# Mask sums of the mLSTM heads from GpSimd to VectorE, and another order of VectorE's work in a head

## The reference, cut to what matters

```python
b = jnp.cumsum(fc, axis=-1)
dmat = jnp.where(lower, b[..., :, None] - b[..., None, :] + ic[..., None, :], NEG)
...
w_intra = jnp.exp(dmat - m_t[..., None])
w_inter = jnp.exp(inter - m_t)
s = jnp.einsum('bhtd,bhsd->bhts', qc, kc) * w_intra
num = w_inter[..., None] * jnp.einsum('bhtd,bhde->bhte', qc, C) + jnp.einsum('bhts,bhse->bhte', s, vc)
den = w_inter * jnp.einsum('bhtd,bhd->bht', qc, n) + jnp.sum(s, axis=-1)
h = num / jnp.maximum(jnp.abs(den), jnp.exp(-m_t))[..., None]
...
C_new = decay[..., None, None] * C + jnp.einsum('bhs,bhsd,bhse->bhde', w_state, kc, vc)
```

## Time and profile before

| | |
|---|---|
| median of 3 runs | 1091.32 us (1090.98 to 1092.84) |
| profiled execution, its own time | 1088.49 us |
| its span in the trace | 1086.7 us |
| PE busy | 976.1 us (90%) |
| DVE busy | 634.8 us (58%) |
| ACT busy | 496.0 us (46%) |
| POOL busy | 163.8 us (15%) |
| mean granted TensorE clock | 0.956 |
| mLSTM loop (first values of head 0 to the block U) | 291.48 to 425.88 us |

### The profile page before, as it was taken

How to read it: one execution, slowest core, us unless ns; L and a number is a source line. 1 busy time by engine, 2 the same in 40 slices (tenths; PEclk the granted TensorE clock), 3 DMA queues, 4 the chain that set the end, 5 groups by cost and what they waited for, 6 DMA issues and landing times.

```text
span 1086.7 us, 14384 instructions
## 1 busy us (share of the span) xinstructions
PE 976.1 (90%) x5874; PEld 869.9 (80%) x5874; DVE 634.8 (58%) x781; ACT 496.0 (46%) x632; POOL 163.8 (15%) x151
## 2 busy tenths in 40 slices
PE   6799999999888787999999999982999999999960
PEld 2378888899888787999998998882788888888850
DVE  0645643322566767232215444536599999999986
ACT  3354343411445354222124123223578787787753
POOL 3000000010413110696000000001011111111120
PEclk9899999999989899999999999995899999999995
DMA  9735444421523303232221124521999999999945
GB/s 346 305 117 184 166 155 176 143 99 40 143 96 89 96 20 117 103 141 87 79 78 43 74 78 172 234 92 67 356 378 412 423 410 422 406 421 414 396 182 207
DMA packets 36065, 216.40 MB, mean 199 GB/s; under 512 B 4352, under 2 KB 4800, under 8 KB 15520
## 3 DMA queue, kind: packets, MB, share of 16 engines
q1 hardware_dynamic: 27024, 180.23, 42.6%
q0 software_dynamic: 8112, 32.53, 8.7%
q10 hardware_dynamic: 864, 2.73, 0.6%
HBM read 200.68 MB, written 14.79 MB: 198 GB/s over the span
## 4 chain that ended last, share of the span: by engine, by line
PE 82%; DVE 7%; DMA 5%; issue 2%; ACT 2%; SPq 0%; DVEq 0%; ACTq 0%; POOL 0%; POOLq 0%
PE ps L1505 79%; DMA rowA<-yscr 2%; DMA raw<-in_wst 2%; PE ps L1890 1%; DVE cs L1116 1%; DMA yscr<-yb,slot_rows 1%; ACT owh L695 1%; DVE xr L1483 1%; DVE rowB L1480 1%; DVE hn L970 1%; PE ps L1908 1%; DMA xg<-h2scr,slot_rows 1%; DVE hlo L983 0%; DVE hn L988 0%; DVE xr L1487 0%
## 5 line engine op out<-in xcount | busy, mean ns | idle before, releaser
L944 DVE TENSOR_TENSOR wlo<-raw,whi 128x2048 fp32r<-128x2048 f32 x37 | 85.7, 2318 | 145.9 <-ACT whi L595 145.9
L1505 PE MATMUL ps<-hhi,whi 128*128 128x320 f32 x672 | 153.8, 310 | 1.7 <-ACT gF L632 1.7
L1505 PE MATMUL ps<-hhi,wlo 128*128 128x320 f32 x672 | 153.1, 309 | 0.0
L1505 PE MATMUL ps<-hlo,whi 128*128 128x320 f32 x672 | 153.1, 309 | 0.0
L1505 PEld LDWEIGHTS ps<-hhi,whi 128*128 128x128 f32 x672 | 112.6, 188 | 4.9 <-ACT gF L632 2.0
L1505 PEld LDWEIGHTS ps<-hhi,wlo 128*128 128x128 f32 x672 | 112.4, 188 | 0.0
L1505 PEld LDWEIGHTS ps<-hlo,whi 128*128 128x128 f32 x672 | 112.3, 188 | 0.0
L595 ACT ACTIVATE whi<-raw 128x2048 fp32r<-128x2048 f32 x37 | 70.5, 1907 | 85.9 <-PE ps L1505 83.7
L1380 DVE TENSOR_TENSOR wlo<-raw,whi 128x2048 fp32r<-128x2048 f32 x32 | 72.6, 2289 | 5.6 <-ACT whi L871 5.5
L1380 DVE TENSOR_TENSOR olo<-raw,ohi 128x2048 fp32r<-128x2048 f32 x32 | 72.4, 2287 | 4.6 <-ACT ohi L871 4.6
L553 POOL DMA_INDIRECT xg<-h2scr,slot_rows x16 | 18.4, 1149 | 361.7 <-DVE slot_rows L1433 244.9
(11 more groups left out here) (342 smaller groups left out, 2253.7 us busy)
## 6 DMA issues: line engine op xcount, KB each, us to landing
raw<-in_wexp SPq DMA_DIRECT2D x64, 1024.0 KB, 8.6
raw<-in_wst SPq DMA_DIRECT2D x60, 1024.0 KB, 5.1
eraw<-in_wexp SPq DMA_DIRECT2D x32, 1024.0 KB, 7.5
nm<-negscr POOLq DMA_DIRECT2D x8, 640.0 KB, 7.5
wib<-wiscr POOLq DMA_DIRECT2D x8, 512.0 KB, 6.4
xT<-in_x SPq DMA_DIRECT2D x4, 640.0 KB, 11.1
xr<-in_xt SPq DMA_DIRECT2D x1, 2560.0 KB, 9.7
h2scr<-ht ACTq DMA_DIRECT2D x5, 512.0 KB, 3.0
```

The costliest lines, as they stand in the source:

```text
L944: dve.tensor_tensor(lo[:, :], raw[s][:, :], f32(hi[:, :]), ALU.subtract)\
L1505: return nc.tensor.matmul(out, lhsT, rhs, start=start, stop=stop)
```

## The change

The two mask sums of a head are issued by DVE in place of POOL. In DVE's loop `chunk_states(h + 1)` stands directly behind `scale_queries(h + 1)`, then come the rows of head h, then the masks of head h + 2, the products of head h + 1 and `gate_lo(h + 3)`. POOL's loop holds transfers only, the load of `wib` ahead of the one of `nm`.

```diff
@@ POOL
             gp.dma_start(stC[:, :, :, :], st_d).then_inc(d_st_wp, 16)
-            mask_maxima(0)
             gp.wait_ge(v_free, 6 + N_V * NT)
             load_inter(0)
             load_maxima(1)
             for h in range(1, H):
+                load_inter(h)
                 if h < H - 1:
                     load_maxima(h + 1)
-                mask_maxima(h)
-                load_inter(h)
@@ DVE
+            def mask_maxima(h):
+                dve.wait_ge(d_nm[h % 2], 16 * (h // 2 + 1))
+                if h:
+                    dve.wait_ge(s_exp, 2 * h)
+                for d in range(2):
+                    neg = cst[:, (C_NEGF, C_NEGB)[d]:(C_NEGF, C_NEGB)[d] + P]
+                    dve.tensor_tensor(nmd[:, d, :].rearrange("p (t n) -> p t n", n=P),
+                                      nm[h % 2][:, d, :].rearrange("p (t n) -> p t n", n=P),
+                                      by(neg.unsqueeze(1), [P, NT, P]), ALU.add).then_inc(s_mask, 1)
...
             dve.wait_ge(s_gtok, 1)
+            mask_maxima(0)
             for t in range(NT):
                 value_rows(3, t)
             products(0)
             scale_queries(0)
             chunk_states(0)
+            mask_maxima(1)
             gate_lo(2)
             for h in range(H):
                 if h < H - 1:
                     scale_queries(h + 1)
-                    products(h + 1)
-                    gate_lo(h + 3)
                     chunk_states(h + 1)
                 for t in range(NT):
                     head_rows(h, t)
+                if h < H - 2:
+                    mask_maxima(h + 2)
+                if h < H - 1:
+                    products(h + 1)
+                    gate_lo(h + 3)
```

More of the change, by code:

```diff
@@ L460, in load_inter @@
                              .partition_broadcast(P)).then_inc(d_wib, 16)
[L462 to L471, removed]
             load_maxima(0)
```

## The result

The changed kernel takes 1055.89 us (median of 4 runs, 1050.32 to 1057.19) against 1091.38 us of the kernel before (4 runs, 1090.98 to 1092.84): the ratio is 0.9663, with a 95% interval of 0.9627 to 0.9699. It is faster by about 35 us. The profiled execution took 1055.19 us with a span of 1053.4 us; before, these were 1088.49 and 1086.7 us. Between the two profiled executions the gain is 33.3 us.

A forecast was written before the change was run, and what follows sets the result against it. PE was bound by waits for `cs`, held behind `gate_lo` and ACT. Six heads 29.5 us plus tail 2.15 gave 31.7 us: profiled 1088.49 to 1056.8, median 1091.32 to 1059.6; range 1056.5 to 1067.

The forecast's parts named there:

- the last term of the sum: From profiled time to median: the profiled 1056.8 us, with 2.83 us more for the median, becomes 1059.6.
- A head without the stall: PE's time per head in the loop: 13.27 us from tile 2's restart plus 1.34, 14.61 us in place of 19.53.
- Step 1: DVE, states ahead of products and `gate_lo`: states end at 14.9 us, before tile 2 of the next values, 1 us to spare.
- Step 2: DVE's loop with the masks, 1.56 us for two: 13.6 us against PE's 14.61, so it fits.
- Step 3: ACT behind the later masks: weighted keys done at 10.9 us, needed by PE's `states` at 11.5, 0.6 us of room.
- Steps 4 and 5: Products behind DVE's rows are hidden by 4.6 us; POOL's loads of `wib` and `nm` are both hidden.
- Step 6: Tail from the values of head 6 to `U`: 15.05 us against 17.20, with PE idle some 3.9 us.
- The half clock: PE's stretches at 1.2 GHz after stalls: about 6.6 of the 29.5 us gained in six heads.
- A: Rival: DVE's or ACT's ring becomes the bound, partial gain, 1067 us; chance 0.11.
- B: Rival: PE's clock keeps falling, four of six heads keep a slow stretch of 1.64 us, 1066 us; chance 0.06.
- C: Rival: the stall reappears at another wait (`s_p`, `st_free` or `wib`), heads stay near 19.5 us, 1091 us; chance 0.01.
- D: Rival: slower, DVE's loop passes 19.53 us, the old length of a head, 1102 us; chance 0.02.

The follow-up runs named there:

- a_order_only: DVE's new order (states, rows, products, `gate_lo`) with the masks still on POOL, against the kernel before: 1057.85 us, ratio 0.9707.
- c_order_only: The new DVE order with masks still on POOL, run again on another chip, against the kernel before: 1054.41 us, ratio 0.9679.
- a_masks_only: Masks moved to DVE behind the rows, the rest of DVE's program in the old order, against the kernel before: 1089.31 us, ratio 0.9995.
- b_gate_behind: The kernel before with only `gate_lo` moved, behind the rows; masks stay on POOL: 1064.04 us, ratio 0.9782.
- b_tail: The changed kernel with the products of head 7 ahead of the rows of head 6: 1055.00 us, ratio 0.9691 to the kernel before.
- b_masks_twice: The changed kernel with each mask sum made twice: 1058.85 us, ratio 0.9738 to the kernel before.
- a_after_again: The changed kernel, unchanged, run again beside the kernel before: 1055.05 us, ratio 0.9676.
- a_before_again: The kernel before, unchanged, timed against itself: 1089.24 us, ratio 1.000.
- sets a and c: Runs whose labels begin with a or c, each set taken together on its own chip; kernel before 1089.58 us in a, 1089.61 in c.
- b_states_first: The kernel before with the states moved ahead of products and `gate_lo`, all ahead of the rows; masks on POOL: 1068.85 us, ratio 0.9840.

## Why the prediction was right, and where it failed

The mechanism and its places were right. The forecast of 1059.6 was 3.7 us too slow. 2.1 us of that come from the last term of the sum and 1.6 from the sum itself, and the range left only 0.3 us for the second.

- **What bounds the kernel.** Right: a states chain held by `gate_lo` and ACT. a_order_only and c_order_only take nearly the whole gain, a_masks_only takes none, and b_gate_behind shows that moving `gate_lo` alone gives 22.7 us, where b_tail, in the same set, gives 31.8.
- **A head without the stall.** 14.61 predicted, 14.50 measured. The 13.27 us from the restart to the next values hold a first product of 0.49 us in place of 0.39, so the restart was still in it. Six heads: 0.7 us.
- **Step 1.** Right: states ready before tile 2, no wait for `cs`.
- **Step 2.** Right: masks 1.55 (1.56 predicted), products 1.55, 1.0 us idle a head as worked out; with the masks doubled DVE becomes the bound. The contended price is real where both engines sum at once (b_gate_behind), and the change takes it away.
- **Step 3.** Right: 0.6 us of room predicted, 0.6 measured, and b_masks_twice uses it up.
- **Steps 4 and 5.** No wait for `s_p` before head 7, nor for `wib` or `nm` inside the loop. The earlier `wib` of head 1, which I put at nothing for PE, matters only where the masks stay on POOL: in a_order_only its lateness, together with the slow `qd`, costs 1.5 us.
- **Step 6.** 15.05 predicted, 14.97 measured (16.24 and 15.09 in two more traces); the gap on PE 3.9 predicted, 3.80 measured; the clock fell behind it. The 0.3 us for the clock is partly luck: in a_after_again, where it fell at once (0.79 over the tail), the tail was 1.3 us longer, and b_tail kept 1.00 through a gap of 3.02.
- **What comes later** moved as a whole: from `U` to the last expert product 619.81 us before and 619.20 after, 0.6 us less.
- **The step that failed.** "It lies 2.83 below the median of the runs, 1091.32, which would become 1059.6." This took the difference between one execution and the median of three for something that the kernel keeps. It does not: the profiled execution lay 0.2 us below the median in a_before_again and 0.7 below it in the changed kernel (1055.19 and 1055.89). So 2.1 of the 3.7 us are this term. The later medians of the kernel before, 1089.58, 1089.24 and 1086.77 on one chip and 1089.61 on another, are all below 1091.32; from 1089.6 the same sum gives 1057.9, still 2.0 above the measured 1055.89. How much of the high 1091.32 is chance and how much the chip or the hour stays open.
- **The sum and the range.** 31.7 us predicted, 33.3 between the two profiled executions: 0.7 from the heads (14.61 for 14.50), 0.1 in the tail, 0.3 from an earlier start of head 0 and 0.6 from behind `U`. The last two are no part of the change: in a_before_again head 0 starts at 290.86 and the stretch behind `U` is 619.1 us. The lower end of the range, 1056.5, already set the term of 2.83 to nothing (1088.49 - 31.7 = 1056.8), so what put the time 0.6 us outside it is that it left 0.3 us for an error of the sum and for the scatter; executions of the changed kernel lie between 1050.32 and 1057.19.
- **The half clock.** The slow stretches were read from one trace in which four of six heads had one. Another trace has five, one of them longer, and its loop takes 119.40 us. So the 30.2 us that the first trace gives for the six heads (117.20 - 87.00) are 2.2 short of what that execution pays. The medians of sets a and c give a gain of 34.4 to 34.5 us where the two profiled executions give 33.3. That the clock makes this difference is argued, not shown.
- **Rivals.** A's mechanism is real (b_masks_twice), but the change does not reach it. B fell: granted clock 1.00 through six heads. C and D did not come.

What stays open: which of the two landings of the last scatter an execution gets, and why; and why the clock falls after some stalls of 3.56 us and not after others.

## What to carry to other kernels

On an engine that works through its program in order, put first what the bounding engine waits for, and behind it what waits for a third engine; look at both ends of the list, since moving the states alone gave 17.9 us (1086.77 to 1068.85, b_states_first), and moving the products and `gate_lo` behind the states and the rows gave 31.7 (1089.58 to 1057.85, a_order_only, on the same chip). Moving work to a nearly full engine is free only up to the room in its loop, here 1.0 us in 14.5, so measure the room with a doubled cost. And ask how much the time scatters before a range is drawn tighter than that: the first median, of three runs, was 1091.32 us, and later ones of 7 to 23 runs were 1086.77 to 1089.61.

## What was not expected of the hardware

- Stalls of 3.56 us on PE (4.26 in head 0) were followed by a stretch at 1.2 GHz in four of six heads in one trace and in five in another of the same kernel; one of 2.65 us, in head 0 of b_gate_behind, was too (granted clock 0.91). Stalls of 1.2 to 1.8 us were not: b_gate_behind has a granted clock of 1.00 from 309 to 390 us with five of 1.26 to 1.28, b_states_first from 290 to 400 us with eight of 1.18 to 1.79.
- The last scatter of expert rows landed in 3.41 us in one execution and in 7.45 in another of the same kernel, and the span behind the last product of the experts was longer by 4.4 us, of which these are 4.0.
